# Folding the second norm's modulation into the router's weights in a two-layer hybrid backbone on one Trainium2 core

## The reference, cut to what matters

```python
h = rms_norm(x, p["norm1_g"][l]) * (1 + sc1) + sh1
y, states = mixer_block(h, s0, rope, lb_all[l], l, p)      # ends with y @ w_out, w_out 1024 x 1024
x = x + g1 * y
h = rms_norm(x, p["norm2_g"][l]) * (1 + sc2) + sh2
x = x + g2 * expert_choice_ffn(h, p["w_router"][l], ...)

def expert_choice_ffn(h, w_router, w_gate, w_up, w_down):
    aff = softmax(h @ w_router)            # w_router 1024 x 16
    gate, idx = top_k(aff per expert, 2 * N // 16)
    ...

def rms_norm(x, g):
    return x * rsqrt(mean(x * x) + 1e-6) * g
```

## Time and profile before

| | |
|---|---|
| three runs | 2888.27, 2879.00, 2887.17 us; median 2887.17 |
| profiled execution | 2886.46 us |
| its span in the trace | 2884.3 us |
| PE busy | 2606.0 us, 90% |
| DVE busy | 1294.0 us, 45% |
| ACT busy | 625.6 us, 22% |
| POOL busy | 655.4 us, 23% |
| granted TensorE clock, mean | 0.941 |
| mix stage of layer 0 | from 739.5 to 952.3 us of the span |
| mix stage of layer 1 | from 2142.5 to 2357.1 us |

### The profile page before, as it was taken

The page is one execution under the profiler, slowest core; times in us unless marked ns, Lnnn a source line. Parts: engine busy times, 40 slices in busy tenths (PEclk is TensorE's granted clock), DMA queues, the critical chain, the costliest instruction groups (busy, mean ns, idle before and its releaser), DMA issues.

```text
span 2884.3 us, 43390 instructions
## 1 busy us (share of the span) xinstructions
PE 2606.0 (90%) x16540; PEld 1925.8 (67%) x16540; DVE 1294.0 (45%) x2726; ACT 625.6 (22%) x1298; POOL 655.4 (23%) x740
## 2 busy tenths in 40 slices
PE   3999989999899499999969999999999956999994
PEld 1555566665565299999935566566655536999994
DVE  2455545556775612222125554555577743222222
ACT  1233322112211112112123332221121101121121
POOL 0000013444542012122100000444464401112111
PEclk8999999999899599999989999999999977999997
DMA  8433331212543778788643333211144345778774
GB/s 285 155 103 103 110 123 55 82 70 82 200 140 105 279 254 290 262 278 291 206 156 103 105 123 112 89 61 72 63 184 157 113 168 191 275 262 292 277 242 148
DMA packets 223146, 480.63 MB, mean 167 GB/s; under 512 B 26318, under 2 KB 78238, under 8 KB 220574
## 3 DMA queue, kind: packets, MB, share of 16 engines
q1 hardware_dynamic: 205502, 422.12, 41.2%
q0 software_dynamic: 11264, 37.76, 5.1%
q10 hardware_dynamic: 6240, 18.87, 1.8%
HBM read 395.07 MB, written 83.64 MB: 166 GB/s over the span
## 4 chain that ended last, share of the span: by engine, by line
PE 78%; DVE 9%; issue 4%; DMA 3%; SPq 3%; ACT 2%; POOL 1%; POOLq 1%; DVEq 0%; ACTq 0%
PE bank L813 22%; PE bank L846 18%; PE bank L857 9%; PE bank L820 7%; PE bank L784 6%; PE bank L906 6%; DVE work L1522 5%; PE bank L1010 3%; ACT work L1225 2%; PE bank L921 1%; PE bank L1144 1%; SPq L499 1%; PE bank L1061 1%; PE bank L800 1%; DMA work<-x_d 1%
## 5 line engine op out<-in xcount | busy, mean ns | idle before, releaser
L813 PE MATMUL bank<-work 128*128 128x512 f32 (+1 forms) x1728 | 740.5, 576 | 23.1 <-ACT work L1225 12.7
L813 PEld LDWEIGHTS bank<-work 128*128 128x128 f32 x1728 | 319.7, 193 | 341.8 <-issue 304.6
L1225 ACT ACTIVATE work<-bank 128x256 f32<-128x256 f32 (+6 forms) x716 | 285.7, 432 | 1084.2 <-PE bank L846 318.4
L846 PE MATMUL bank<-work 128*128 128x144 f32 x4096 | 511.6, 287 | 2.2 <-DVE work L1522 2.2
L846 PEld LDWEIGHTS bank<-work 128*128 128x128 f32 x4096 | 507.9, 191 | 3.0 <-issue 2.4
L1522 DVE TENSOR_TENSOR work<-work 128x256 f32<-128x256 f32 (+3 forms) x629 | 361.1, 603 | 191.3 <-PE bank L1010 104.2
L784 PE MATMUL bank<-cst,work 128*128 128x128 f32 (+3 forms) x1888 | 253.1, 284 | 139.6 <-DVE work L1982 36.3
L1225 ACT ACTIVATE work<-work 128x256 f32<-128x256 f32 (+3 forms) x247 | 169.1, 685 | 805.1 <-DVE work L1522 495.4
L784 PEld LDWEIGHTS bank<-cst,work 128*128 128x128 f32 (+3 forms) x1888 | 213.0, 144 | 185.1 <-issue 48.5
L1522 DVE TENSOR_TENSOR work<-bank,work 128x144 f32<-128x144 f32 (+2 forms) x218 | 90.1, 420 | 509.2 <-ACT work L1225 501.7
L906 PE MATMUL bank<-work 128*128 128x512 f32 x576 | 264.0, 612 | 5.3 <-ACT work L1225 2.2
(11 more groups left out here) (153 smaller groups left out, 2144.1 us busy)
## 6 DMA issues: line engine op xcount, KB each, us to landing
work<-in_w_gate_dram SPq DMA_DIRECT2D x32, 2048.0 KB, 8.4
work<-in_w_up_dram SPq DMA_DIRECT2D x32, 2048.0 KB, 13.3
work<-in_w_down_dram SPq DMA_DIRECT2D x32, 2048.0 KB, 12.3
work<-in_w_ada_dram SPq DMA_DIRECT2D x32, 1024.0 KB, 5.9
work<-sum_d SPq DMA_DIRECT2D x18, 1024.0 KB, 5.0
work<-in_w_ada_dram SPq DMA_DIRECT2D x8, 2048.0 KB, 12.8
work<-in_w_in_dram SPq DMA_DIRECT2D x8, 2048.0 KB, 15.7
hT_d<-work SPq DMA_DIRECT2D x18, 512.0 KB, 3.6
```

Of the source, the lines that this page charges most:

```text
L813: mm = pe.matmul(bank[:, bk, 0:w.shape[-1]], h[:, ch, :], w[:, ch, :], start=(ch == 0), stop=(ch == DC - 1))
L846: mm = pe.matmul(bank[:, 4 + f, o:o + CAP_S + CAP_P], w[:, ch, f * P:(f + 1) * P], e_xt[:, ch, :], start=(ch == 0), stop=(ch == DC - 1))
L1225: return act.activation(out, in_, func, **kw)
```

## The change

- The router's weights are built once a layer, in `router_weights` (DVE, behind tile 4 of the local stage): `w_rm[:, ch, 0:16]` is `w_r` times the context scale, `w_rm[:, ch, 16:32]` times the latent scale, and `w_rc` holds the sums of `w_r` times the shifts. The four small instructions of `spread` for scale2 and shift2 move there from the start of the mix stage.
- `turn_x1` turns the residual sum `r_x1`, without its root, and ACT copies it out plainly (`take_x1`, two instructions of 128x512). `modulated` is gone.
- `router` has `w_rm` (128x32) as the weights and `r_ht` (128x128) as the moving operand, with the chunks spread over four column groups. The 128x128 result is copied by ACT (`take_part`), and `router_rows` adds the four groups and turns it, with one matmul of 128x16. In the first step one matmul with `ones` spreads the constant.
- `logits` (DVE) multiplies by `small[:, 2:3]` and adds the constant, in one instruction.
- `project(n, 1)` is split in two: chunks 0 to 3, then `router(n-1)`, then chunks 4 to 7, then `router_rows(n-1)`.
- `second_norm` stays for the store to `xn_d`, and PE no longer waits for it. `turn_x1` waits for `r_x1` and for the second step of `mix_states` of the tile that shares banks 0 and 7.

```diff
+            def turn_x1(n, free):
+                pe.wait_ge(sem["r_x1"], by("r_x1", n))
+                if free:
+                    pe.wait_ge(sem["r_o"], by("r_o", free, 2))
                 for half in range(2):
                     for i in range(4):
                         ch = half * 4 + i
-                        mm = turn(bank[:, 7 * half, i * P:(i + 1) * P], r_xn[:, ch * P:(ch + 1) * P])
+                        mm = turn(bank[:, 7 * half, i * P:(i + 1) * P], r_x1[:, ch * P:(ch + 1) * P])
                     mm.then_inc(sem["r_xT"], 1)
             def router(n):
+                pe.wait_ge(sem["r_ht"], by("r_ht", n, 1))
+                for ch in range(DC):
+                    g = ch % 4
+                    mm = pe.matmul(bank[32 * g:32 * g + 32, 1, 0:P], w_rm[:, ch, :], r_ht[:, ch, :], start=(ch < 4), stop=(ch >= 4))
+                mm.then_inc(sem["r_lg"], 1)
+            def router_rows(n, kind):
                 pe.wait_ge(sem["r_ht"], by("r_ht", n))
-                for ch in range(DC):
-                    mm = pe.matmul(bank[:, 1, 0:NE], r_ht[:, ch, :], w_r[:, ch, :], start=(ch == 0), stop=(ch == DC - 1))
-                mm.then_inc(sem["r_lg"], 1)
+                if kind == 0:
+                    pe.matmul(bank[:, 1, 2 * P:2 * P + 2 * NE], ones, w_rc[:, :, :].rearrange("p k e -> p (k e)"), start=True, stop=True)
+                pe.matmul(bank[:, 1, 3 * P:3 * P + NE], r_part, cst[:, C_PICK + NE * kind:C_PICK + NE * (kind + 1)], start=True, stop=True).then_inc(sem["r_lg"], 1)
...
                     project(n, 0)
-                    turn_xn(n - 1)
-                    project(n, 1)
+                    turn_x1(n - 1, n + 2 if j + 2 < NT else None)
+                    project(n, 1, 0, 4)
                     if j >= 2:
                         pe.wait_ge(sem["r_lgc"], by("r_lgc", n - 2))
                     router(n - 1)
-                turn_xn(l * NT + NT)
+                    project(n, 1, 4, 8)
+                    router_rows(n - 1, int(j > 1))
+                turn_x1(l * NT + NT, None)
                 pe.wait_ge(sem["r_lgc"], by("r_lgc", l * NT + NT - 1))
                 router(l * NT + NT)
+                router_rows(l * NT + NT, 1)
...
+            def take_x1(n):                                        # ACT
+                for half in range(2):
+                    act.wait_ge(sem["r_xT"], by("r_xT", n, half + 1))
+                    act.wait_ge(sem["r_lg"], before("r_lg", n))
+                    last = ev(r_ht[:, 4 * half:4 * half + 4, :], bank[:, 7 * half, :].rearrange("p (a b) -> p a b", a=4))
+                last.then_inc(sem["r_ht"], 1)
+            def take_part(n):                                      # ACT
+                act.wait_ge(sem["r_lg"], by("r_lg", n, 1))
+                ev(r_part, bank[:, 1, 0:P]).then_inc(sem["r_ht"], 1)
...
                     squares_x(n - 1)
+                    take_x1(n - 1)
                     if j + 2 < NT:
                         squares_o(l, j + 2)
+                    take_part(n - 1)
...
             def logits(t, n):                                      # DVE
+                kind = int(t > 0)
                 dve.wait_ge(sem["r_lg"], by("r_lg", n))
-                dve.tensor_copy(lg_all[:, t, :], bank[:, 1, 0:NE]).then_inc(sem["r_lgc"], 1)
+                if t == 0:
+                    step(dve.tensor_copy(lg_add[:, :, :].rearrange("p k e -> p (k e)"), bank[:, 1, 2 * P:2 * P + 2 * NE]))
+                dve.scalar_tensor_tensor(out=lg_all[:, t, :], in0=bank[:, 1, 3 * P:3 * P + NE], scalar=small[:, 2:3], in1=lg_add[:, kind, :],
+                                         op0=ALU.mult, op1=ALU.add).then_inc(sem["r_lgc"], 1)
+            def router_weights(nl):                                # DVE
+                step(spread(24, 8, scale2, shift2))
+                products = lg_all[:, :, :].rearrange("p t e -> p (t e)")[:, 0:NE * DC].rearrange("p (e c) -> p e c", c=DC)
+                for k in range(2):
+                    tt(w_rm[:, :, NE * k:NE * (k + 1)], w_r[:, :, :], bc(scale2[:, k, :], NE))
+                    step(tt(products, w_r[:, :, :].rearrange("p c e -> p e c"), shift2[:, k, :].unsqueeze(1).broadcast_to([P, NE, DC])))
+                    step(dve.tensor_reduce(w_rc[:, k, :], products, AX, ALU.add))
```

More of the change, by code:

```diff
@@ L68 @@
 C_PICK = C_RT + 4
-C_RM = C_PICK + 2
+C_RM = C_PICK + 32
 C_RQ = C_RM + 4 * P
@@ L110, in shape_constants @@
             c[:, C_SIN + tile * 64 + j * 32:][:, :32] = si * sc
-    for j in range(2):
+    for j in range(32):
         c[:, C_PICK + j] = i % 32 == j
@@ L173, in trunk @@
         lg_all = sb("lg_all", [P, NT, NE])
-        WORK = 48024
+        w_rm = sb("w_rm", [P, DC, 2 * NE])
+        w_rc = sb("w_rc", [P, 2, NE])
+        lg_add = sb("lg_add", [P, 2, NE])
+        WORK = 47672
         work = sb("work", [P, WORK])
@@ L320, in trunk @@
         r_step = take(8, HD)
+        r_part = take(P)
         s_diag = [v.rearrange("p (a b) -> p a b", b=P) for v in (r_gy, r_xn, r_junk)] + [r_ht]
@@ L900, in turn_y, with project @@
                     mm.then_inc(sem["r_yT"], 1)
-            def project(n, half):
+            def project(n, half, c0=0, c1=DC):
                 pe.wait_ge(sem["r_yt"], by("r_yt", n))
                 pe.wait_ge(sem["r_gy"], before("r_gy", n))
-                for ch in range(DC):
+                for ch in range(c0, c1):
                     mm = pe.matmul(bank[:, 5 + half, :], r_yt[:, ch, :], r_w[:, ch, half * 512:(half + 1) * 512], start=(ch == 0), stop=(ch == DC - 1))
-                mm.then_inc(sem["r_out"], 1)
-            def turn_xn(n):
-                pe.wait_ge(sem["r_xn"], by("r_xn", n))
+                if c1 == DC:
+                    mm.then_inc(sem["r_out"], 1)
+            def turn_x1(n, free):
+                pe.wait_ge(sem["r_x1"], by("r_x1", n))
+                if free:
+                    pe.wait_ge(sem["r_o"], by("r_o", free, 2))
                 for half in range(2):
@@ L1485, in _ @@
                     squares_x(n - 1)
+                    take_x1(n - 1)
                     if j + 2 < NT:
                         squares_o(l, j + 2)
+                    take_part(n - 1)
                 squares_x(l * NT + NT)
+                take_x1(l * NT + NT)
+                take_part(l * NT + NT)
                 barrier(act, l, 4)
@@ L1835, in gated @@
                 dve.wait_ge(sem["r_ss"], before("r_ss", n))
+                dve.wait_ge(sem["r_xT"], before("r_xT", n))
                 tt(r_x1, r_x, r_gy, ALU.add).then_inc(sem["r_x1"], 1)
@@ L1839, in second_norm @@
                 dve.wait_ge(sem["r_rs2"], by("r_rs2", n))
-                dve.wait_ge(sem["r_xT"], before("r_xT", n))
                 dve.wait_ge(sem["r_nst"], before("r_nst", n))
                 dve.tensor_scalar(r_xn, r_x1, small[:, 2:3], None, ALU.mult).then_inc(sem["r_xn"], 1)
-            def modulated(t, n):
-                for ch in range(DC):
-                    if ch % 4 == 0:
-                        dve.wait_ge(sem["r_xT"], by("r_xT", n, ch // 4 + 1))
-                        dve.wait_ge(sem["r_lg"], before("r_lg", n))
-                    last = dve.tensor_scalar(r_ht[:, ch, :], bank[:, 7 * (ch // 4), (ch % 4) * P:(ch % 4 + 1) * P],
-                                             scale2[:, t, ch:ch + 1], shift2[:, t, ch:ch + 1], ALU.mult, ALU.add)
-                last.then_inc(sem["r_ht"], 1)
             def logits(t, n):
+                kind = int(t > 0)
                 dve.wait_ge(sem["r_lg"], by("r_lg", n))
-                dve.tensor_copy(lg_all[:, t, :], bank[:, 1, 0:NE]).then_inc(sem["r_lgc"], 1)
+                if t == 0:
[9 more added lines that the diff above has]
+                    step(dve.tensor_reduce(w_rc[:, k, :], products, AX, ALU.add))
             for l in range(DEPTH):
@@ L1907, in _ @@
                     tile_l(l, t, l * NT + t + 1)
+                    if t == 4:
+                        router_weights(nl)
                 barrier(dve, l, 3)
@@ L1912, in _ @@
                     diagonal(i, nl)
-                spread(24, 8, scale2, shift2)
                 mix_states(l, 1)
@@ L1935, in _ @@
                         mix_gate(l, j + 2)
-                    modulated(MIX[j - 1], n - 1)
                     if j + 2 < NT:
@@ L1941, in _ @@
                 second_norm(l * NT + NT)
-                modulated(MIX[NT - 1], l * NT + NT)
                 logits(MIX[NT - 1], l * NT + NT)
@@ L2095, in residual @@
             def residual(n):
-                rstd(0, 1, 2, "r_ss", "r_rv2", "r_rs2", "r_xn", n)
+                rstd(0, 1, 2, "r_ss", "r_rv2", "r_rs2", "r_lgc", n)
             for l in range(DEPTH):
```

3 lines of the change are left out of this document (1 added, 2 removed).

## The result

The changed kernel takes 2852.47 us (four runs, 2846.87 to 2854.68), the kernel before 2887.19 (four runs, 2879.00 to 2888.27). The ratio is 0.9886, 95% interval 0.9868 to 0.9904. The profiled execution takes 2854.68 us with a span of 2852.6, which is 31.7 us less than the span before.

What follows compares the result with a forecast made beforehand. PE was taken to bound the mix steps, nearly level with a DVE chain. Per layer 6.1 + 1.2 - 0.2 + 4.75 = 11.85 us, both 23.7; from 2886.46 that gave 2862.8, stated as 2863, range 2855 to 2875.

Steps and rivals of the forecast that it cites:

- the clock: Steps 7 and 8 of the mix stage: slow projections may go, up to 5.1 us, or new ones come; counted as nothing.
- these drops: Three projections behind ACT's copy gap, layer 0 step 7 and layer 1 steps 7 and 8: 8.8 us, not 7.1.
- Rival 2: The clock drops in steps 7 and 8 go as well: 2858 us, chance 17%.
- The router: On PE in the mix loop: 1.70 us replaced by 0.73 plus rows 0.21, 0.76 less each, 6.1 a layer.
- The straight line through 512 and 256 columns: Router matmul time on PE extrapolated from 1.85 and 1.00 us to 0.575 at 128 columns.
- Rivals 1, 3 and 4: Router on PE: stays at 1.00 us, 2870 (16%); gains nothing, 2879 (9%); array emptied for every record, 2923 (4%).
- The wait for the norm: PE's wait for second_norm before the turns goes: 0.25 us in four steps, 0.16 in step 1, 1.2 a layer.
- So at least 1.4 us of cover are left: Mix steps: the turns' new inputs are ready by 806.85 at the latest, PE reaches the turns at 808.3.
- ACT's order: Copies moved to ACT in each mix step stay covered by half projections of 3.4 us on PE; counted as nothing.
- The stage's end: Mix stage end: turns start with the last sum, xn_d store about level; 4.75 us less, between 3.0 and 5.2.
- The weights: Preparation on DVE, some 5 us in the local stage, hidden in a 10.36 us idle stretch; no cost, no gain.

Runs made afterwards that it cites:

- Experiments 1 to 4: Kernel before with its old router mid-projection 2881.77 us; changed kernel without column groups 2867.09 and 2869.86, with a light block 2863.42, with the block doubled 2879.56.
- the two sets of runs: The changed kernel measured twice without edits: 2852.47 us (ratio 0.9886), then again 2856.69 us (0.9904).
- Experiment 2: Changed kernel with folded weights kept but no column groups or router_rows; router mid-projection 2867.09 us, or behind the projection 2869.86 us.
- the late router: Changed kernel without column groups or router_rows, its router behind the whole second projection: 2869.86 us, ratio 0.9950.
- experiment 1: Kernel before with only its own router moved to the middle of the second projection: 2881.77 us, ratio 0.9992.
- experiment 5: Changed kernel with the second projection undivided, router and router_rows behind it: 2857.68 us, ratio 0.9906.
- experiment 4: Changed kernel with sixteen unused matmuls of the old router's shape ending steps 6 and 7 of each layer: 2879.56 us, ratio 0.9975.

## Why the prediction came out as it did

**The step that failed** is the one on the clock: "Some of these drops may go, up to 5.1 us in all; in the same way new ones may fall elsewhere. The forecast counts neither." All three went, none came, in each of the changed kernel's two profiles: 1.70 + 1.67 + 1.67 = 5.0 of the 7.2 us by which the stages gained more than the 23.7 forecast. So the term that was put at nothing, the drops' going, measured 5.0 us in the profiled executions. The facts were in the rows: each drop had the old router, eight transposes and the gap ahead, and the change took the router out of that row of light work, leaving 1.95 of 3.5 us. Experiments 1 to 4 show in their traces that this is the cause of the drops' going: moving the old router away ends the drops, putting its like back brings them again in two of four places, twice of it in all four. Rival 2 named the event and got 17%, because step 8 of layer 0 had the same work and no drop. That was read as "it hangs on more than that". It was right, and it says only that the drop isn't certain with such work, not that it stays without it.

**The range** was narrow on this side. Rival 2 alone gives 2858, its better bounds 2855; the time lies at 2852 to 2857 by the two sets of runs, and the gain over the kernel before is 34.7 us in the first and 28.6 in the second, where 24 were said. The profiled execution, 2854.68, is 8.1 us below the sum of 2862.8: 5.0 are the drops, 2.2 the rest of the stages, 0.8 all else. The last 2.2 us down to the median are the spread of executions, which was no term of the range. On which side of 2855 a median fell is luck in part: 2852.47 in one set, 2856.69 in the other.

**The router** was right: 0.73 said, 0.57 + 0.20 = 0.77 measured; rows 0.21 said, 0.14 measured; net 0.76 said, 0.79 measured. The straight line through 512 and 256 columns gave 0.575 at 128. Experiment 2 gives 0.84 a step for the same thing (0.80 with the late router). Rivals 1, 3 and 4 are out by the row of 0.57. The Trainium skill names about 62 ns per MATMUL as a floor where the sequencer decodes in ucode (TensorE: Matmul & The Clock Gate, Wait — 56ns, not 53.3ns?). An estimate from that figure is 16 x 62 ns, 0.99 us; this trace has 0.57 / 16 = 36 ns a record. The Trainium skill's rule that a change of tiling mode drains the array (TensorEngine Tiling (Array Packing), Key Properties) fits the 0.20 us for going in and out here, of which dividing the projection is no part (experiment 1).

**The wait for the norm** was right and somewhat small: 1.2 us a layer said. Steps 2 to 5 fell from 82.50 to 78.09 us, 1.10 each where 1.01 was said. The turns themselves cost 0.87 from start to start where they cost 0.93 behind a wait, and the router gave 0.03 more. "So at least 1.4 us of cover are left" held: no idle ahead of any turn.

**ACT's order** held. There is no gap ahead of the router or of the rows in any step of the loop, and experiment 5 shows what the cover is worth: without it 0.47 us a step.

**The stage's end** was right in its mechanism, place and size: 4.75 us said, 5.0 measured. The turns start within 0.1 us of the sum, the store is issued at 935.89 and holds the barrier, its transfer taking 2.56 us (2.7 said). The clock there was 0.64 and not 0.5, since PE's first turns ran at full rate, so the logits came 1.4 us ahead of the landing where they were said to be about level. The landing times of all stores are as before:

```profile
DMA to landing us min/median/max: 2.6/3.4/4.3
```

**The weights** cost nothing, as said, and `spread`'s going brought nothing: DVE stands in its place now, waiting for PE (timeline of DVE, start of the mix stage; see the earlier trace rows).

```profile
750.53 0.75 DVE L1554 TENSOR_TENSOR work<-work,bank 128x256 f32<-128x256 f32 x2 [2.86 <-PE bank L889]
```

In the local stage they ran at 618.9 to 623.0 us, one tile behind the idle stretch shown in the earlier trace rows; the mix stage starts at 740.42, not 739.64, inside the spread of the other kernels. The 2.2 us of the difference that the clock leaves are step 1 (1.1 and 1.0 us shorter where 0.7 was said), the ends (0.5 in all), and some 0.1 in each of the steps 2 to 5.

## What to carry to other kernels

Where a row of dense matmuls has a place that runs partly at half rate behind a short gap, count the narrow and turning work that stands right ahead of it, and price its removal as a case of its own; an operation may be worth more by leaving that place than by its own length. A folded scale pays here through the wait that it removes at the end of a stage, and the store that stays behind becomes the next bound, so ask for it too whether the barrier needs it. Two points with the same layout gave the time of a third width within 0.01 us here.

## What the runs showed of the hardware

- Eight matmuls with 32-column weights in four column groups and 128 moving columns, float32, take 0.57 us in a dense row. The same product with the roles exchanged and 16 moving columns takes 1.70.
- Going in and out of the column groups in the middle of a projection costs 0.20 us together (7.07 against 6.87).
- The clock fell without any gap, under narrow work alone (experiment 4: 1.95 us for transposes that otherwise take 1.07, straight behind 3.5 us of matmuls with 16 moving columns). A projection of 7.13 us behind a short gap that ran slow took 8.7 to 9.0, in two places 10.1.
- The same instructions behind the same work ran slow in one step and not in another of one execution, and the projection behind step 1's gap took anything from 7.4 to 9.1 us.
